# Split products that read and write pairs of columns from two halves, extra unread products, and two moved vector steps

## What is computed

```python
def first_block(x, c, ...):
    for l in range(DEPTH):                       # 2
        h = rmsnorm(x, g_mix_pre[l]) * (1.0 + scale_a) + shift_a
        y = hybrid_mixer(h, w_in[l], ...)
        x = x + gate_a * rmsnorm(y, g_mix_post[l])
        h = rmsnorm(x, g_ffn_pre[l]) * (1.0 + scale_f) + shift_f
        x = x + gate_f * rmsnorm(swiglu(h, w_gate_up[l], w_down[l]), g_ffn_post[l])

def second_block(x, ...):
    for i in range(DEPTH_2):                     # 4
        h = h + 0.5 * rmsnorm_2(swiglu_2(rmsnorm_2(h, gn[0]), ...), gn[1])
        m = (hgrn2_mixer, diff_attention, pool_mixer)[i % N_MIXERS](rmsnorm_2(h, gn[2]), ...)
        h = h + rmsnorm_2(m, gn[3])
        h = h + 0.5 * rmsnorm_2(swiglu_2(rmsnorm_2(h, gn[4]), ...), gn[5])
```

## Time and profile before

| | us |
|---|---|
| runs | 2685.79, 2684.87, 2684.28 |
| median | 2684.87 |
| the profiled execution | 2684.98 |
| its span, first to last instruction | 2683.2 |

### The profile page before, as it was taken

The page is one execution under the profiler, slowest core; times in us unless marked ns, Lnnn a source line. Parts: engine busy times, 40 slices in busy tenths (PEclk is TensorE's granted clock), DMA queues, the critical chain, the costliest instruction groups (busy, mean ns, idle before and its releaser), DMA issues.

```text
span 2683.2 us, 41968 instructions
## 1 busy us (share of the span) xinstructions
PE 2616.6 (98%) x16461; PEld 2350.8 (88%) x16461; DVE 1777.6 (66%) x2172; ACT 1389.3 (52%) x1931; POOL 254.6 (9%) x387
## 2 busy tenths in 40 slices
PE   7899999999999999999999899999999999999998
PEld 6789998899888998888889788888988888898887
DVE  6858865564666876666667766666666666687665
ACT  3654446633544665445445554554554454575543
POOL 4231011100100121000000100000010000022000
PEclk8999999999999999999999999999999999999999
DMA  9549944375555444555554365555555555554553
GB/s 368 198 139 370 347 159 135 127 251 183 194 193 192 157 145 159 195 188 182 188 192 159 110 214 191 172 202 190 179 195 188 192 192 188 173 165 138 177 188 125
DMA packets 349406, 509.61 MB, mean 190 GB/s; under 512 B 9413, under 2 KB 302364, under 8 KB 345180
## 3 DMA queue, kind: packets, MB, share of 16 engines
q1 hardware_dynamic: 344080, 494.89, 53.6%
q0 software_dynamic: 4384, 12.00, 1.3%
q10 hardware_dynamic: 812, 0.91, 0.1%
HBM read 505.93 MB, written 1.84 MB: 189 GB/s over the span
## 4 chain that ended last, share of the span: by engine, by line
PE 86%; DVE 6%; ACT 3%; issue 2%; DMA 1%; POOL 1%; DVEq 0%; ACTq 0%; SPq 0%
PE B L637 20%; PE B L638 10%; PE Y L600 9%; PE Y L602 9%; PE Y L601 9%; PE B L600 8%; PE B L601 7%; PE B L602 7%; DVE w_lo L2006 1%; ACT w_hi L1442 1%; ACT junk L1453 1%; DMA M<-in_w_ada 1%; DVE M L2016 1%; ACT h_both L1523 0%; PE B L1094 0%
## 5 line engine op out<-in xcount | busy, mean ns | idle before, releaser
L2006 DVE TENSOR_TENSOR w_lo<-raw,w_hi 128x2048 fp32r<-128x2048 f32 (+1 forms) x412 | 937.1, 2275 | 238.1 <-ACT w_hi L1442 238.0
L1442 ACT ACTIVATE w_hi<-raw 128x2048 fp32r<-128x2048 f32 (+1 forms) x425 | 804.1, 1895 | 438.3 <-PE B L638 258.8
L637 PE MATMUL B<-h_both,w_hi 128*128 128x512 f32 x2304 | 806.6, 393 | 0.0
L638 PE MATMUL B<-h_both,w_lo 128*128 128x256 f32 x2304 | 647.7, 281 | 0.0
L637 PEld LDWEIGHTS B<-h_both,w_hi 128*128 128x128 f32 x2304 | 432.7, 188 | 95.3
L638 PEld LDWEIGHTS B<-h_both,w_lo 128*128 128x128 f32 x2304 | 433.4, 188 | 2.7
L600 PE MATMUL B<-h_both,w_hi 128*128 128x256 f32 x1356 | 385.1, 284 | 1.1 <-DVE w_lo L2006 0.8
L601 PE MATMUL B<-h_both,w_hi 128*128 128x256 f32 x1356 | 382.1, 282 | 0.0
L602 PE MATMUL B<-h_both,w_lo 128*128 128x256 f32 x1356 | 381.9, 282 | 0.0
L2016 DVE TENSOR_TENSOR xn<-B,xn 128x256 f32<-128x256 f32 (+1 forms) x296 | 114.4, 427 | 345.5 <-ACT xn L1447 337.2
L600 PE MATMUL Y<-w_hi,a_hi 128*128 128x512 f32 x812 | 319.3, 393 | 0.0
(11 more groups left out here) (376 smaller groups left out, 3516.2 us busy)
## 6 DMA issues: line engine op xcount, KB each, us to landing
raw<-in_ffn_w_in SPq DMA_DIRECT2D x176, 1024.0 KB, 5.0
raw<-in_ffn_w_out SPq DMA_DIRECT2D x88, 1024.0 KB, 4.8
raw<-in_w_gate_up SPq DMA_DIRECT2D x44, 1024.0 KB, 5.5
M<-in_w_ada SPq DMA_DIRECT2D x37, 1024.0 KB, 8.7
raw<-in_hgrn_w_in SPq DMA_DIRECT2D x32, 1024.0 KB, 5.3
raw<-in_w_down SPq DMA_DIRECT2D x22, 1024.0 KB, 4.9
raw<-in_w_in SPq DMA_DIRECT2D x14, 1024.0 KB, 6.4
raw<-in_diff_w_in SPq DMA_DIRECT2D x12, 1024.0 KB, 5.0
```

The source lines that it names most:

```text
L637: pe.matmul(B[banks[c]], hi[:, s], h_both[:, k, :, :].rearrange("p a b -> p (a b)"), start=k == 0, stop=False)
L638: mm = pe.matmul(B[banks[c]][:, 0:S], lo[:, s], h_hi[:, k, :], start=False, stop=k == KD - 1)
L1442: act.activation(w_hi[st.n % RING][:, 0:n], raw[st.r % RING][:, 0:n], ACT.Copy).then_inc(unit_rounded, 1)
L2006: dve.tensor_tensor(w_lo[s][:, 0:n], raw[st.r % RING][:, 0:n], w_hi[s][:, 0:n].bitcast(F32), ALU.subtract).then_inc(unit_split, st.step("" ...
```

## The change

It has five parts.

1. `paired(v)` is a view of the same memory in another order: of n columns it takes 0 and 1, then n/2 and n/2 + 1, then 2 and 3, and so on. `mm3`, `stationary_wide` and `by_tokens` now use it for the moving operand and the output of every split product. Both sides use the same order, so each result lands in the cell where it landed before. Stationary operands and all other products are as before.
2. `outputs(0)` on DVE moves from step 7 of `mixer1` to the head of step 6, ahead of `mac_of(5)`, in both layers.
3. `lo_of("out3")` in layer 0 moves from the end of step 14 to step 15, behind `maxima(15)`.
4. `idle_products` are added in waits of `mixer1` (6 in each layer), `hgrn` (8 in each of two), `diff` (6 and 7).
5. `probe_forms` adds 30 unread split products behind TensorE's last product, three of each of ten forms: 512 or 256 columns, output plain or in pairs, input plain, in pairs, in fours, in every second column, or column by column from two or four parts.

```diff
@@ -595,8 +595,13 @@
             st = steps(pe, tensor_step, {unit_multiplied.name: RING})
             pe.sem_inc(unit_multiplied, RING)
 
+            def paired(v):
+
+                return v.rearrange("p (a n two) -> p n a two", a=2, two=2)
+
             def mm3(o, lh, ll, rh, rl, first, last):
 
+                o, rh, rl = paired(o), paired(rh), paired(rl)
                 pe.matmul(o, lh, rh, start=first, stop=False)
                 pe.matmul(o, lh, rl, start=False, stop=False)
                 return pe.matmul(o, ll, rh, start=False, stop=last)
@@ -634,8 +639,8 @@
                         halfway()
                     for k in range(KD):
                         s = slice(k * CH + c * P, k * CH + c * P + P)
-                        pe.matmul(B[banks[c]], hi[:, s], h_both[:, k, :, :].rearrange("p a b -> p (a b)"), start=k == 0, stop=False)
-                        mm = pe.matmul(B[banks[c]][:, 0:S], lo[:, s], h_hi[:, k, :], start=False, stop=k == KD - 1)
+                        pe.matmul(paired(B[banks[c]]), hi[:, s], h_both[:, k, :, :].rearrange("p a (n two) -> p n a two", two=2), start=k == 0, stop=False)
+                        mm = pe.matmul(paired(B[banks[c]][:, 0:S]), lo[:, s], paired(h_hi[:, k, :]), start=False, stop=k == KD - 1)
                 mm.then_inc(unit_multiplied, st.step(name, unit_multiplied))
 
             def moving(os, name, n, lh, ll, kt, stride, halfway=None):
@@ -785,18 +790,18 @@
 
                 def work(w, t, ready, part=None, ks=range(KD)):
                     hi, lo = w
-                    out = o[:, t * n:t * n + n]
+                    out, whole = paired(o[:, t * n:t * n + n]), o[:, t * n:t * n + n]
                     for k in ks:
                         if ready and k % part_of(ready) == 0:
                             pe.wait_ge(vector_step, st.at(f"{ready}.h{t}.{k // part_of(ready)}"))
                         s, rows_of = slice(k * n, k * n + n), slice(t * P, t * P + P)
                         if part == "rounded":
-                            pe.matmul(out, h_hi[:, k, rows_of], hi[:, s], start=k == 0, stop=False)
-                            mm = pe.matmul(out, h_lo[:, k, rows_of], hi[:, s], start=False, stop=False)
+                            pe.matmul(out, h_hi[:, k, rows_of], paired(hi[:, s]), start=k == 0, stop=False)
+                            mm = pe.matmul(out, h_lo[:, k, rows_of], paired(hi[:, s]), start=False, stop=False)
                         elif part == "rest":
-                            mm = pe.matmul(out, h_hi[:, k, rows_of], lo[:, s], start=False, stop=k == KD - 1)
+                            mm = pe.matmul(out, h_hi[:, k, rows_of], paired(lo[:, s]), start=False, stop=k == KD - 1)
                         else:
-                            mm = mm3(out, h_hi[:, k, rows_of], h_lo[:, k, rows_of], hi[:, s], lo[:, s], k == 0, k == KD - 1)
+                            mm = mm3(whole, h_hi[:, k, rows_of], h_lo[:, k, rows_of], hi[:, s], lo[:, s], k == 0, k == KD - 1)
                     return mm
                 return work
 
@@ -882,6 +887,20 @@
 
                 into_y_pair(p, (f"{p}.last.down", f"{p}.end.down"), ((a_hi, a_lo), (h_hi, h_lo)), False, True,
                             last_inputs)
+
+            def probe_forms():
+
+                a, b = w_hi[0], w_hi[1]
+                alternating = lambda v: v.rearrange("p (two n) -> p n two", two=2)
+                four = lambda v: v.rearrange("p (a n four) -> p n a four", a=2, four=4)
+                plain = lambda v: v
+                forms = ((512, plain, plain), (512, plain, alternating), (512, plain, paired), (512, paired, paired),
+                         (512, plain, lambda v: v.rearrange("p (n two) -> p two n", two=2)), (512, plain, four),
+                         (256, plain, plain), (256, plain, alternating), (256, paired, paired),
+                         (512, plain, lambda v: v.rearrange("p (q n) -> p n q", q=4)))
+                for n, (w, to, by) in enumerate(forms):
+                    for i in range(3):
+                        pe.matmul(to(B[n % 4][:, 0:w]), a[:, i * P:i * P + P], by(b[:, 0:w]), start=i == 0, stop=i == 2)
 
             def mixer1(l):
                 p = f"M{l}"
@@ -1053,6 +1072,9 @@
                     dense(s)
                     if s < 16:
                         scores(s)
+                    if s == 17:
+                        pe.wait_ge(vector_step, st.at(f"{p}.m14"))
+                        idle_products(6, B[0])
                     if 2 <= s < 18:
                         turn(s - 2)
                     if s >= 3:
@@ -1109,6 +1131,9 @@
                 def scores(c):
 
                     bi, bx, bs = (0, 2, 3) if c == 3 else (4, 6, 7)
+                    if c == 3:
+                        pe.wait_ge(st.sem_of(f"{p}.f3.ev"), st.at(f"{p}.f3.ev"))
+                        idle_products(8, B[0])
                     pe.wait_ge(vector_step, st.at(f"{p}.qk{c}"))
                     if c == 3:
                         for e in "qfvg":
@@ -1306,9 +1331,13 @@
                         scores(s)
                     if 2 <= s < 18:
                         turn(s - 2)
+                    if s == 16:
+                        pe.wait_ge(vector_step, st.at(f"{p}.m14"))
+                        idle_products(6, B[0])
                     if s >= 3:
                         values(s - 3)
                     if s == 16:
+                        idle_products(7, B[0])
                         turn_pair(2)
                 out_tile(1, 1)
                 out_tile(2, 0, lambda: turn_pair(3))
@@ -1429,6 +1458,8 @@
                 ffn(f"{i}a")
                 (hgrn, diff, pooling)[i % 3](f"{i}m")
                 ffn(f"{i}b")
+
+            probe_forms()
 
 
         @block.scalar
@@ -2432,9 +2463,9 @@
                         move_keys(1)
                         mac_of(4)
                     elif s == 6:
+                        outputs(0)
                         mac_of(5)
                     elif s == 7:
-                        outputs(0)
                         move_keys(2)
                     elif s == 8:
                         normed("fox")
@@ -2456,8 +2487,8 @@
                             mac_of(7)
                     elif s == 14:
                         outputs(2)
-                        if l == 0:
-                            lo_of("out3")
+                    elif s == 15 and l == 0:
+                        lo_of("out3")
                     elif s == 16:
                         normed("mla")
                 outputs(3)
```

## The result

The changed kernel takes 3620.67 us (3619.58 to 3621.16) against 2684.57 us for the kernel before (2683.10 to 2685.79), measured beside it: ratio 1.3488, 95% interval 1.3466 to 1.3509. I had forecast 2673.5 us with a range of 2560 to 2840. That is wrong by 947 us, far outside the range.

What follows compares the result with a forecast made beforehand. The prediction took TensorE's split products, and the interval between their starts, as the bound. Its terms, 0 - 3.2 - 2.2 + 0 - 6 + 0 = -11.4 us against 2684.98, gave 2673.5 us, range 2560 to 2840.

Steps and rivals of the forecast that it cites:

- Term (1): Split products on TensorE, read and written in pairs: interval between starts unchanged, 0 us.
- Doubled: Upper bound for pairs on split products: more moves in memory double the time above full rate, +165 us.
- the excess: Time split products take above full rate: some 0.015 us per wide and 0.009 per narrow one, 165 us in all.
- excess grows: Rival on split products: changing place every two columns costs more at full rate; doubled, 2838 us; chance 0.22.
- two steps: Rival on split products: pairs too short to feed the stream, two clock steps a column, +2000 us, 4670 us; chance 0.14.
- Term (2): First block's mixer, both layers: outputs(0) earlier on DVE removes TensorE waits of 1.75 and 1.41 us, -3.2 us.
- Term (3): Mixer layer 0: out3's split behind the last maxima starts the chain TensorE waits for 2.2 us earlier, -2.2 us.
- Term (4): Mixer, hgrn and diff waits: 41 unread products keep the clock up; half of 12.3 us taken, -6 us.
- Term (5): End of TensorE's program: 30 unread products take 5.9 us, nobody waits for them, 0 us.

Runs made afterwards that it cites:

- e2_plain: The changed kernel with its split products in plain order again, all other edits kept: 2672.57 us, ratio 0.9956.
- e4_input_pairs: The changed kernel with pairs in the moving operand alone, outputs written in plain order: 3621.74 us, a single execution.
- e1_forms: The kernel before plus 26 forms of 12 unread products at its end, differing in operand or result pattern: wide plain 232 ns, pairs read 327, halves taken singly 216.
- e5_line_order: The changed kernel without pairs, streamed weights stored so natural column order reads places 0, 4, 1, 5, 2, 6, 3, 7 of each eight: 2628.97 us, ratio 0.9801.
- e8_h_in_turns: e5_line_order with h_both at the wide gate and up products also read from two halves in turn: 2582.27 us, ratio 0.9618.
- e7_forms_2: The kernel before plus twelve more forms of 12 unread products at its end, in other reading orders: mean steps from 216 to 461 ns.
- e3_output_pairs: The changed kernel with pairs in the output alone, moving operand read in plain order: 2672.92 us, ratio 0.9958.
- e6_moves_alone: The kernel before with only outputs(0) moved ahead and out3's split moved later: 2676.26 us, ratio 0.9975.
- e9_no_unread_at_end: e8_h_in_turns without the 30 unread products at the end: 2582.32 us, ratio 0.9618.

## Why the prediction was wrong, step by step

**Term (1), the pairs: 0 expected, 948 us measured (e2_plain to the changed kernel; 949 to e4_input_pairs).** This is the step that failed: the interval of the split products was taken as unchanged, and it went from 231 to 328 ns and from 118 to 165. It failed in three places. First, the row that I took the zero from. L1138 against L1140 has runs of 16 columns, which lie in whole groups of four, and I compared record lengths (268 and 275 ns), which say nothing of what a product costs. By the starts both rows step by 112 ns (median), while 64 columns at two steps a column are 53: the row has slack for twice its reading. It could not show a cost of runs of two, as I wrote, and I took its side all the same. Second, the bounds. "Doubled" was a number without a mechanism: the excess of a wide product grew from 15 to 112 ns, more than sevenfold. Two steps a column was the f32 rows' rate, which belongs to another kind of product; split products come near it only where every own column of a reader lies in fresh 16 bytes (453 ns). The measured 1.53 steps lie between, at 2684.87 + 936, and no case of mine covered it. Third, the sum of chances: *excess grows* and *two steps* held 0.36 together, and both say that this stream has no slack; the range should have run through the gap between them, since all that was known was that the price is somewhere between nothing and two steps. Of the argument for *excess grows* one half was right: this stream has no slack at the full rate, and the excess of 15 ns is the price of the order in which it reads, since in another order it is gone (e1_forms, e5_line_order, e8_h_in_turns). The other half, that changing place more often costs more, was wrong: two halves taken singly change place at every column and take 216 ns, pairs change half as often and take 327.

**The rule of the Trainium skill** in "Advanced Engine Details and Errata", Memory Cachelines. For SBUF it asks for two hits on a line of 16 bytes. The pairs of the change have exactly two, and cost 41%; form (4) of e7_forms_2, two neighbours of each four and no return, takes 454 ns. What decides in most of these forms, in the picture inferred above, is how many of *its own* columns each of two alternating readers finds in the 16 bytes: with one, 327 or 453 ns; with two, 232 (243 to 250 in eights and fours of two halves); with four, 216. For PSUM the same section says that any non-contiguous pattern slows matmuls; e3_output_pairs and the forms with results in pairs and in fours (232, 233) show no cost, so for results its second sentence, two neighbours together, held.

**Term (2), `outputs(0)` earlier, -3.2 us.** Both waits went, as predicted. But I had said that what comes next isn't late, and in layer 0 it was. TensorE in e2_plain, layer 0, against the earlier trace rows:

```profile
117.50 0.89 PE L973 MATMUL B<-M 96*128 96x128 f32 x4 [0.88 <-issue]
...
125.13 1.42 PE L973 MATMUL B<-M 96*128 96x128 f32 x4 [2.79 <-DVE M L2044]
```

and the same place in the kernel before:

```profile
125.46 0.89 PE L954 MATMUL B<-M 96*128 96x128 f32 x4 [1.70 <-DVE M L2013]
...
129.50 0.85 PE L975 MATMUL B<-M 128*128 128x64 f32 x6 [0.93 <-DVE xn L2016]
130.86 0.47 PE L600 MATMUL Y<-w_hi,h_both 128*128 128x512 f32 x1 [0.51 <-DVE h_both L2401]
```

The waits of 1.75, 1.70, 0.93 and 0.51 became 0.88 and 2.79: 1.2 us less in layer 0. Layer 1 lost its 1.41, but a new wait of 0.71 us for DVE's h_both stands at 482.45 (0.70 in e6_moves_alone, so it isn't the products in the waits that bring it). Right in sign, 1.9 instead of 3.2 us, and behind the longer wait the clock was at 1.2 GHz for longer (below).

**Term (3), `out3`'s split later, -2.2 us.** In e6_moves_alone, where no products fill it, the wait of 3.78 us is this:

```profile
145.17 0.52 PE L967 MATMUL B<-ident,M 128*128 128x128 f32 x3 [1.72 <-ACT M L1452]
```

2.06 us less. Right. Together with (2), 5.4 us expected and 6.7 (4.3 to 9.1) measured; the waits alone account for 4.0 of it, so that the two numbers lie so close is in part luck.

**Term (4), products in waits, -6 us.** The 41 products are there (L707, 166 records in 20.6 us instead of the 84 in 10.3 us of the earlier trace rows), and behind all four waits the granted clock is 1.00, where it was 0.50; in the profile of e2_plain it doesn't fall again after 135.6 us. The same stretches of e2_plain (its program runs 1 to 12 us ahead of the one before):

```profile
148.70:155.00 6.30, 5.59 (x29) 4.41 (x28) 3.53 (x8) 4.51 (x9) 0.89 (x2) 1.00 0.24 83
482.90:486.10 3.20, 3.20 (x18) 2.63 (x17) 2.89 (x3) 0.96 (x2) 0.00 (x0) 1.00 0.00 0
1001.70:1011.60 9.90, 9.34 (x49) 7.58 (x49) 6.82 (x15) 3.18 (x12) 1.01 (x1) 1.00 0.44 139
1517.00:1523.50 6.50, 6.22 (x28) 4.92 (x27) 4.07 (x5) 1.20 (x3) 0.75 (x2) 1.00 0.40 135
```

I had taken half of 12.3 us; 5.1 us were measured, though known to 4 us only. Two things stand against reading this as more than it is. In e2_plain the 11 us behind the new 2.79 us wait (125 to 136) have a mean clock of 0.53, where the kernel before had 0.57 for 4 us (131 to 135). And e6_moves_alone, without one of these products, also lost the low clock of layer 1 and of the first hgrn layer, and had one in the second hgrn layer instead. Its stretches at these three places:

```profile
482.00:487.00 5.00, 5.00 (x24) 4.09 (x25) 3.62 (x5) 2.00 (x3) 0.25 (x1) 1.00 0.05 11
992.00:1002.00 10.00, 7.54 (x65) 7.13 (x63) 7.51 (x16) 6.88 (x13) 1.31 (x2) 1.00 0.58 201
...
2447.00:2458.00 11.00, 11.00 (x56) 11.00 (x57) 6.27 (x12) 4.88 (x11) 0.00 (x0) 0.53 0.36 122
```

Which of like waits is followed by a low clock changes with small shifts of the program. All executions together, not the profiled ones alone, say more: the mean granted clock is 0.994 to 0.997 in all nine of e2_plain and e3_output_pairs, and 0.989 to 0.994 in the eleven of e6_moves_alone. Some 0.001 of that is the end of the program, where without the 30 products the clock falls while TensorE has nothing to do. So the clock is higher in this kernel with the products in the waits than without. Which of the four fillings does it, and that filled waits keep the clock up in general, isn't shown.

**Term (5), the 30 products at the end, 0.** e8_h_in_turns with them and e9_no_unread_at_end without: 2582.27 and 2582.32 us. Right. In the changed kernel they take 7.7 us instead of 5.9, since six forms are slow (333 to 449 ns for pairs and every second column, 256 and 277 for fours and four parts, 171 for narrow pairs), and still end about where the span does, at 3618.9:

```profile
3610.66 0.51 PE L607 MATMUL Y<-w_hi,h_both 128*128 128x512 f32 x1
...
3610.99 7.69 PE L903 MATMUL B<-w_hi 128*128 128x512 f32 x30
```

The last product of the kernel proper starts 8.2 us before the end of the span, as in the earlier trace rows.

**The sum without (1)** was -11.4 us, that is 2673.5; e2_plain gave 2672.57. That they agree to 1 us is in part luck, since (2) brought 1.9 instead of 3.2 and the share of (4) is known to 4 us only. The signs and places of the small terms were read rightly from the trace, and together they are a hundredth of the one that had no row.

## What to carry to other kernels

When a change alters the access pattern of the instruction that bounds the kernel, and no row of the trace has that pattern, the working for all other terms is worth little: keep the range open from nothing to the worst that the same engine shows, or measure a dozen unread products of that form first, which costs some microseconds at the end of a kernel. And take a small excess over the full rate seriously: here 231 against 216 ns was the price of the reading order already. Storing the weights so that neighbouring columns are read from two groups of 16 bytes in turn gave 44 us, and reading the activations from two halves in turn another 47, together most of the 3.8%, with no instruction more.

## What the runs showed of the hardware that I had not expected

- The moving operand of these split products: 216 ns for 512 columns in the orders 0, 4, 1, 5, 2, 6, 3, 7 or 0, 256, 1, 257; 232 in plain order; 327 in pairs of two halves; 453 at every second column; 461 at every fourth. Fours of two halves take 250, eights 243. The distance of the halves (256 to 1024 columns) changed the time of pairs by 5 ns at most.
- A result written in pairs or in fours from two halves costs nothing (232 and 233 ns).
- A stationary operand taken from every second column costs nothing with 512 moving columns in plain order (231 ns, e1_forms) and 2 ns with 256 (120 against 118.5). With 256 columns from two halves in turn it takes 120 too, against 111.6, so there the gain of the reading order is lost.
- VectorE's addition of 128x256 takes 619 ns instead of 419 when its result is written as 0, 128, 1, 129 and both inputs are read in order; its subtraction of 128x2048 with one input at every second place 2294 ns, against 2287 without. ScalarE's copy of 128x2048 with its input at every second place takes 2107 ns, against 1911.
